# Three norm stages of a two-part transformer kernel: the second weight unit of the next block is cast later, and its early pieces move behind the last transpose

## The chip, the cores and the metric

The kernel runs on one core of a Trainium2 chip. The metric is the device time of one execution in microseconds (us), lower being better. A core has a matrix engine (TensorE, in the rows PE, its weight loads PEld), a vector engine (VectorE, DVE), a scalar engine (ScalarE, ACT), a general engine (GpSimd, POOL), and SyncE (SP), whose queue issues the weight loads here.

## The reference, cut to what matters

Everything is float32, one batch of 512 tokens of width 1024. Two layers of a mixed block (gated recurrence, latent attention, cross-attention, layer norm) come first. The second part is one block of this form, and the change lies in it:

```python
f = swiglu(rms_norm(h, ffn1_pre_g[i]), ffn1_w_gate[i], ffn1_w_up[i], ffn1_w_down[i])
h = h + 0.5 * rms_norm(f, ffn1_post_g[i])
m = hybrid_mixer(rms_norm(h, mix_pre_g[i]), w_in[i], ...)
h = h + rms_norm(m, mix_post_g[i])
f = swiglu(rms_norm(h, ffn2_pre_g[i]), ffn2_w_gate[i], ffn2_w_up[i], ffn2_w_down[i])
h = h + 0.5 * rms_norm(f, ffn2_post_g[i])
e = (p[i] @ ple_w_proj[i]) * jax.nn.sigmoid(rms_norm(h, ple_pre_g[i]) @ ple_w_gate[i])
```

After the first feed-forward, after the mixer and after the second feed-forward the same thing happens: the sum over a token's 1024 values is squared and averaged, h is updated, h is squared and averaged again, scaled, and multiplied by the next weights.

## The kernel before, in words

**Matmuls.** A float32 product is made of three matmuls of split operands: each operand is a rounded high part (`xh`, `wh`) and the rest (`xl`, `wl`), and lines 867 to 869 issue high by high, low by high and high by low. Weights come in units of up to four tiles of 128x512. For each unit SyncE loads `raw` (line 797, two buffers, so that the load of unit u waits until the low parts of unit u-2 are made), ScalarE casts the four tiles to `wh` (line 1200, three buffers, so that the cast of unit u waits until TensorE is through with unit u-3), and GpSimd makes `wl` as raw minus wh (line 816, one instruction for each tile). A block of weights of 1024 rows is two units; a piece is one unit by one PSUM bank, 12 matmuls. Only the first piece of a unit waits for the low tiles, one by one.

**Norm stages.** `norm_order` writes out by hand the order in which TensorE, ScalarE and VectorE go through such a stage; a `Phase("norm")` carries it. There are five: mode "layer" closes each of the two layers of the first part, and mode "post" stands behind the first feed-forward, behind the mixer and behind the second feed-forward. The change touches mode "post"; below, the first, second and third stage are these three. For each of the four groups t of 128 tokens it goes: the last two down pieces (`part`) on TensorE, their sum (`evac`, line 1571) and the gain product (`gain`, line 1895) on VectorE, a square with root (`root`, lines 1457 and 1458) on ScalarE, the update of h (`x`, line 1906) on VectorE, a second square with root (`root2`, lines 1464 and 1465) on ScalarE, the scaling in two halves (`n`, line 1914) on VectorE, the transposes of the two halves (`t`, line 1105, four each) on TensorE, and the split of the transposed values into `xh` (`high`, lines 1472 and 1475) and `xl` (`low`, lines 1924 and 1930).

**Pieces ahead.** The block that follows the stage (`next_block`) is begun within it: its pieces over the first 256 tokens need only t = 0 and 1. These are in `early`, eight pieces of 12 matmuls with 256 columns where the block is of kind "tr" (behind the first feed-forward and behind the mixer), and four pieces with 512 columns where it is "nat" (behind the second feed-forward). They are dealt out in three lots (`lots`): behind the last down piece, behind the transposes of t = 2, and behind those of t = 3. I call the block's two units A and B; the first half of `early` uses A, the second half B. The second token half of the block follows, for A and then B again.

**Casts ahead.** `("units", 0)` and `("units", 1)` in ScalarE's order are the casts of A and of B, four tiles each. In ScalarE's order the steps of t = 3 read, before the change: units 1 (B's casts), root 3, high 2, root2 3, high 3.

Of the kernel before, what the change touches and what calls it, by code (L numbers as in the profile page):

```python
# [216 lines left out]
def norm_order(first, pre, turned):  # L217

    last = T - 1
    if not turned:
        pe = [("part", t, n) for t in range(T) for n in range(2)]
        act = [("root", t) for t in range(T)]
        dve = sum(([("evac", t, 0, 2), ("gain", t), ("x", t)] for t in range(T)), [])
    else:
        def turn(t):
            return [("t", t, b) for b in range(2)]

        def high(t):
            return [("high", t, b) for b in range(2)]

        def low(t):
            return [("low", t, b) for b in range(2)]

        def n(t):
            return [("n", t, b) for b in range(2)] if pre else []

        def root2(t):  # L240
            return [("root2", t)] if pre else []

        parts = [[("part", t, b)] for t in range(T) for b in range(2)]
        early = [[("early", i)] for i in range(3)]
        if first == "layer":

            parts = [[("part", t, b)] for t in range(T) for b in range(4 if t == 1 else 2)]
            pe = parts[:7] + [turn(0), parts[7], parts[8], turn(1), parts[9], early[0], turn(2), early[1], turn(3), early[2]]

            def evac(t, a, b):  # L250
                return [("evac", t, a, b)]

            def ready(t):
                return [("stat", t), ("gain", t)]

            def x(t):
                return [("x", t)]

            def root(t):
                return [("root", t)]  # L260

            dve = [evac(0, 0, 2), ready(0), evac(1, 0, 1), x(0), evac(1, 1, 2), n(0), evac(1, 2, 4), ready(1), x(1),
                   evac(2, 0, 1), low(0), n(1), evac(2, 1, 2), ready(2), evac(3, 0, 1), x(2), low(1), evac(3, 1, 2),
                   ready(3), n(2), x(3)]
            dve += [n(3), low(2), low(3)] if pre else [low(2), low(3)]
            act = [root(0), root2(0), [("units", 0)], root(1), high(0), root2(1), root(2), high(1), root2(2), root(3),
                   [("units", 1)], root2(3), high(2), high(3)]
        else:
            pe = parts[:5] + [turn(0), parts[5], parts[6], turn(1), parts[7], early[0], turn(2), early[1], turn(3), early[2]]
            act, dve = [[("units", 0)]], []  # L270
            for t in range(T):
                dve.append([("evac", t, 0, 2)])
                if t:
                    dve.append(n(t - 1))
                dve.append([("gain", t), ("x", t)])
                if t:
                    dve.append(low(t - 1))
                act.append([("units", 1), ("root", t)] if t == last else [("root", t)])
                if t:
                    act.append(high(t - 1))  # L280
                act.append(root2(t))
            dve += [n(last), low(last)]
            act.append(high(last))
        pe, act, dve = (sum(order, []) for order in (pe, act, dve))
    free = ("part", "early", "evac", "units")
    at = [{k: i + 1 for i, k in enumerate(k for k in order if k[0] not in free)} for order in (pe, act, dve)]
    return (pe, act, dve), at


def build(nc, x, x_t, mem_t, positions, w_in, w_uq, w_uk, w_uv, w_mk, w_mv, w_out, ln_g, ln_b, cols_in,  # L290
# [3 lines left out]
    with ctx:  # L294
# [105 lines left out]
        def w_cols(w, row0, ktiles, c0, width):  # L400
            return w[row0:row0 + ktiles * P, c0:c0 + width].rearrange("(k p) n -> p k n", p=P)
# [17 lines left out]
        def norm(first, last_blocks, pre=None, turned=True, scale=1.0, second=True, by_columns=False):  # L419


            _, at = norm_order(first, pre, turned)
            ph = Phase("norm", *(len(o) for o in at), slots=T + 1, writes="x" if turned else None, mode=first,
                       gain=pre, tiles=2 if turned else 0, scale=scale, layer=second)
            ph.by_columns = by_columns
            if len(last_blocks) == 2:
                last_blocks[1].shift = 2
            if first == "layer":

                between, *ends = (b.pieces() for b in last_blocks)  # L430
                for b, at in zip(last_blocks, ((0, 1, 0, 1), (2, 2, 0, 2), (3, 3, 1, 3))):
                    b.shift, b.at = 0, at
                ph.slots[0], ph.slots[2] = between[:2], between[2:]
                for n in range(T):
                    ph.slots[n + 1] += [pieces[n] for pieces in ends]
                add(ph)
                return
            for b in last_blocks:
                pieces = b.pieces()
                ph.slots[0] += pieces[:-T]  # L440
                for n in range(T):
                    ph.slots[n + 1].append(pieces[n - T])
            add(ph)
# [143 lines left out]
        for n in range(2):  # L587
            add(blk2(2048 + 512 * n, "nat", "sigmoid", "act", SG2) if n else rest)
            add(Block(w_cols(w_ba, 0, 4, n * 512, 512), 4, 512, "nat", "y", "merge", "dve", (n, True, SG2)))
            if n == 0:  # L590
# [5 lines left out]
        last = [Block(w_cols(w_out2, k * 512, 4, n * 512, 512), 4, 512, "nat", "x", "accumulate", "dve", (n, k == 0))  # L596
                for k in range(2) for n in range(2)]
# [46 lines left out]
        units, unit_end, bank_user = [], [], {}  # L644
# [67 lines left out]
        for u, (_, _, nk) in enumerate(units):  # L712
            for k in range(nk):
                lows[low_on_dve(u, k)] += 1
                low_at[u, k] = lows[low_on_dve(u, k)]
            low_upto.append(tuple(lows))

        tiles_upto = [0]
        for _, _, nk in units:
            tiles_upto.append(tiles_upto[-1] + nk)  # L720
# [100 lines left out]
        def _(pe):  # L821
# [55 lines left out]
            def half_pieces(b, half):  # L877

                return [pc for pc in b.pieces() if b.kind != "nat" or pc[2] // 2 == half]
# [5 lines left out]
            for e in plan:  # L885
# [142 lines left out]
                elif e.kind == "level" and e.level <= LEVELS:  # L1028
                    for h in range(4):
# [3 lines left out]
                        for c in range(T):  # L1033
# [6 lines left out]
                            for o in range(0, P, 64):  # L1040
                                own = slice(c * P + o, c * P + o + 64)
                                right, n = Q[:, h, own], 64
                                if e.level:
                                    right, n = right.rearrange("p (b two i) -> p b two i", two=2,
                                                               i=2 ** (e.level - 1))[:, :, 1, :], 32
# [19 lines left out]
                elif e.kind == "read_out":  # L1065
                    for c in range(T):
# [6 lines left out]
                        mm.then_inc(pe_step, 1)  # L1073
                elif e.kind == "norm":
                    (order, _, _), (_, act_at, dve_at) = norm_order(e.mode, e.gain, e.tiles)
                    early = half_pieces(e.next_block, 0) if e.tiles else []
                    n = len(early) // 4
                    first = 2 * n if e.mode == "layer" else n
                    lots = early[:first], early[first:3 * n], early[3 * n:]

                    def half_written():

# [3 lines left out]
                    for key in order:  # L1086
                        if key[0] == "part":
                            _, t, n = key
# [7 lines left out]
                        _, t, b = key  # L1096
# [63 lines left out]
        def _(act):  # L1160
# [79 lines left out]
            for e in plan:  # L1240
# [187 lines left out]
                elif e.kind == "hg_norm":  # L1428
                    act.activation(stat[:, 16:32], stat[:, 0:16], ACT.Sqrt, bias=col("eps_rms"),
                                   scale=1 / P).then_inc(act_step, 1)  # L1430
                elif e.kind == "norm":
                    (_, order, _), (pe_at, act_at, dve_at) = norm_order(e.mode, e.gain, e.tiles)
                    squares = square2_out if e.layer else square_out
                    if e.mode == "layer":
# [666 lines left out]
```

## Time and profile before

| what | value |
| --- | --- |
| time, median of 3 runs | 2168.9 us (2168.37 to 2169.25) |
| profiled execution: its own time | 2171.62 us |
| profiled execution: span | 2169.8 us |
| TensorE busy | 2134.5 us, 98% of the span |
| GpSimd busy | 877.0 us, 40% |
| mean granted TensorE clock | 0.997 of full |

The span is from the first to the last instruction of one profiled execution; its own time, 1.8 us longer, has what lies around it. Times in rows are counted from the start of the span. "Idle before" is how long the engine stood before the row and what ended it.

### The profile page before, as it was taken

Reading aid. Unit: us, or ns where it says so; the run is one execution under the profiler, and the core shown is the slowest. Engines: PE = TensorE matmul, PEld = TensorE weight load, DVE = VectorE, ACT = ScalarE, POOL = GpSimd, SP = SyncE. Lnnn points to the kernel's source line nnn. Section 1 sums busy time; section 2 is a strip of 40 time slices with the busy share of each in tenths; the row PEclk is TensorE's granted clock in tenths of the full one; section 3 lists DMA queues with packets and bytes.
Section 4 is the critical chain, followed back from the end, with each engine's and each line's share of the span. In section 5 each row is a group of like instructions: output and inputs, shape, how many; then the busy total and the mean of one; then the engine's idle time right before and its main releaser. Section 6 shows DMA issues by size and latency. Waiting matters only on the chain. (4 is left out here: it accounts for less than half of the span.)

```text
span 2169.8 us, 30402 instructions
## 1 busy us (share of the span) xinstructions
PE 2134.5 (98%) x12268; PEld 1756.7 (81%) x12268; DVE 880.0 (41%) x1669; ACT 787.7 (36%) x1609; POOL 877.0 (40%) x688
## 2 busy tenths in 40 slices
PE   7999999999999999999999999999999999999998
PEld 7888888778888888678888888887788888888876
DVE  6074464535355374534531212353432532222264
ACT  4413325454324224445522222244523432222245
POOL 4533433232443433223453544434354345454433
PEclk9999999999999999999999999999999999999999
DMA  6422222112321212113142322322132223332222
GB/s 244 156 77 79 75 65 94 43 61 77 97 79 59 94 56 68 59 59 107 50 146 78 117 97 78 112 98 88 59 117 97 78 81 123 107 99 97 96 68 87
DMA packets 98667, 196.45 MB, mean 91 GB/s; under 512 B 3680, under 2 KB 12256, under 8 KB 98144
## 3 DMA queue, kind: packets, MB, share of 16 engines
q1 hardware_dynamic: 95072, 183.25, 25.7%
q10 hardware_dynamic: 3456, 11.27, 1.5%
q8 instruction: 97, 1.59, 0.3%
q14 instruction: 42, 0.34, 0.1%
HBM read 192.41 MB, written 2.10 MB: 90 GB/s over the span
## 5 line engine op out<-in xcount | busy, mean ns | idle before, releaser
L816 POOL TENSOR_TENSOR wl<-raw,wh 128x512 fp32r<-128x512 f32 (+2 forms) x684 | 876.8, 1305 | 1265.9 <-ACT wh L1200 1255.9
L1200 ACT CAST wh<-raw 128x512 fp32r<-128x512 f32 (+2 forms) x692 | 380.2, 603 | 768.2 <-PE ps L869 669.8
L867 PE MATMUL ps<-xh,wh 128*128 128x512 f32 (+1 forms) x1376 | 516.2, 375 | 3.9 <-POOL wl L816 2.6
L869 PE MATMUL ps<-xh,wl 128*128 128x512 f32 (+1 forms) x1376 | 509.9, 371 | 0.0
L868 PE MATMUL ps<-xl,wh 128*128 128x512 f32 (+1 forms) x1376 | 509.5, 370 | 0.0
L867 PEld LDWEIGHTS ps<-xh,wh 128*128 128x128 f32 x1376 | 260.1, 189 | 50.5 <-issue 4.6
L869 PEld LDWEIGHTS ps<-xh,wl 128*128 128x128 f32 x1376 | 259.9, 189 | 44.6
L868 PEld LDWEIGHTS ps<-xl,wh 128*128 128x128 f32 x1376 | 260.2, 189 | 42.1
L867 PE MATMUL ps<-wh,xh 128*128 128x512 f32 (+1 forms) x608 | 240.1, 395 | 0.2 <-issue 0.2
L869 PE MATMUL ps<-wh,xl 128*128 128x512 f32 (+1 forms) x608 | 234.8, 386 | 0.0
L868 PE MATMUL ps<-wl,xh 128*128 128x512 f32 (+1 forms) x608 | 234.7, 386 | 0.0
L867 PE MATMUL ps<-wh,yh 128*128 128x512 f32 x496 | 199.6, 402 | 2.1 <-DVE side L1555 2.0
L869 PE MATMUL ps<-wh,yl 128*128 128x512 f32 x496 | 194.4, 392 | 0.0
L868 PE MATMUL ps<-wl,yh 128*128 128x512 f32 x496 | 194.2, 392 | 0.0
L1575 DVE TENSOR_TENSOR work<-ps,work 128x512 f32<-128x512 f32 x44 | 30.3, 688 | 381.1 <-PE ps L869 381.1
L867 PEld LDWEIGHTS ps<-wh,xh 128*128 128x128 f32 x608 | 114.2, 188 | 23.3 <-issue 1.9
L869 PEld LDWEIGHTS ps<-wh,xl 128*128 128x128 f32 x608 | 114.2, 188 | 21.7
L868 PEld LDWEIGHTS ps<-wl,xh 128*128 128x128 f32 x608 | 114.3, 188 | 20.4 <-issue 0.2
L867 PEld LDWEIGHTS ps<-wh,yh 128*128 128x128 f32 x496 | 93.9, 189 | 22.4 <-ACT xh L1289 2.1
L869 PEld LDWEIGHTS ps<-wh,yl 128*128 128x128 f32 x496 | 93.6, 189 | 20.0
L868 PEld LDWEIGHTS ps<-wl,yh 128*128 128x128 f32 x496 | 93.6, 189 | 18.4
L1571 DVE TENSOR_TENSOR side<-side,ps 128x512 f32<-128x512 f32 x88 | 59.3, 686 | 106.0 <-PE ps L869 103.4
(261 smaller groups left out, 2460.6 us busy)
## 6 DMA issues: line engine op xcount, KB each, us to landing
raw<-w_in SPq DMA_DIRECT2D x58, 1024.0 KB, 5.2
raw<-w_out SPq DMA_DIRECT2D x20, 1024.0 KB, 5.1
raw<-f1g SPq DMA_DIRECT2D x10, 1024.0 KB, 5.1
raw<-f1u SPq DMA_DIRECT2D x10, 1024.0 KB, 5.1
raw<-f1d SPq DMA_DIRECT2D x10, 1024.0 KB, 5.1
raw<-f2g SPq DMA_DIRECT2D x10, 1024.0 KB, 5.1
raw<-f2u SPq DMA_DIRECT2D x10, 1024.0 KB, 5.1
raw<-f2d SPq DMA_DIRECT2D x10, 1024.0 KB, 5.1
```

Source lines behind the costliest of these rows:

```text
L816: pool.tensor_tensor(wl[s], raw[:, u % 2, k, 0:b.width], wh[s].bitcast(F32), ALU.subtract).then_inc(low_done, 1)
L867: pe.matmul(o, still[0], move[0], start=k0 + k == 0, stop=False)
L868: pe.matmul(o, still[0], move[1], start=False, stop=False)
L869: mm = pe.matmul(o, still[1], move[0], start=False, stop=k0 + k == b.ktiles - 1)
L1200: act.copy(wh[:, v % 3, k, 0:width], raw[:, v % 2, k, 0:width]).then_inc(high_done, 1)
L1571: ins = dve.tensor_copy(dst, src) if first else dve.tensor_tensor(dst, dst, src, ALU.add)
L1575: link(dve.tensor_tensor(tmp, src, SG[:, j, :], ALU.mult))
```

## The change

In mode "post", B's casts go from ahead of root 3 to behind root2 3, directly ahead of high 3. The lots of `early` were one, two and one quarters of the pieces and are now one, one and two quarters: all of B's pieces stand behind the transposes of t = 3. Mode "layer" keeps its order and its lots.

```diff
-                act.append([("units", 1), ("root", t)] if t == last else [("root", t)])
+                act.append([("root", t)])
                 if t:
                     act.append(high(t - 1))
                 act.append(root2(t))
             dve += [n(last), low(last)]
-            act.append(high(last))
+            act += [[("units", 1)], high(last)]
...
                     first = 2 * n if e.mode == "layer" else n
-                    lots = early[:first], early[first:3 * n], early[3 * n:]
+
+                    second = 3 * n if e.mode == "layer" else 2 * n
+                    lots = early[:first], early[first:second], early[second:]
```

## Rows read from the trace of the kernel before

**Rows 1.** The page: busy us by engine; one costly group (busy us, mean ns)

```profile
PE 2134.5 (98%) x12268; PEld 1756.7 (81%) x12268; DVE 880.0 (41%) x1669; ACT 787.7 (36%) x1609; POOL 877.0 (40%) x688
...
L1571 DVE TENSOR_TENSOR side<-side,ps 128x512 f32<-128x512 f32 x88 | 59.3, 686 | 106.0 <-PE ps L869 103.4
```

**Rows 2.** Waits of TensorE, whole span: us in total, times, longest

```profile
PE ps L1105 <- DVE work L1914: 4.5, 6, 1.0
```

**Rows 3.** Timeline, first stage, ScalarE: start us, duration us, instruction, [idle before]

```profile
1424.17 0.29 ACT L1465 ACTIVATE stat<-stat,cols 128x1 f32<-128x1 f32 x1
1424.37 2.17 ACT L1200 CAST wh<-raw 128x512 fp32r<-128x512 f32 x4
1433.07 1.06 ACT L1464 ACTIVATE work<-xs 128x1024 f32<-128x1024 f32 x1 [3.08 <-DVE xs L1906]
1434.25 0.29 ACT L1465 ACTIVATE stat<-stat,cols 128x1 f32<-128x1 f32 x1
```

**Rows 4.** Timeline, first stage, VectorE, t = 2, then t = 3

```profile
1420.34 1.22 DVE L1895 TENSOR_TENSOR work<-side,work 128x1024 f32<-128x1024 f32 x1
...
1421.67 1.28 DVE L1906 SCALAR_TENSOR_TENSOR xs<-work,stat,xs 128x1024 f32<-128x1024 f32 x1
...
1426.82 1.77 DVE L1914 SCALAR_TENSOR_TENSOR work<-xs,stat,work 128x512 f32<-128x512 f32 x1
1428.51 2.29 DVE L1895 TENSOR_TENSOR work<-side,work 128x1024 f32<-128x1024 f32 x1
...
1430.92 2.12 DVE L1906 SCALAR_TENSOR_TENSOR xs<-work,stat,xs 128x1024 f32<-128x1024 f32 x1
```

**Rows 5.** Timeline, first stage, GpSimd: one low tile, four, the next four

```profile
1426.30 1.74 POOL L816 TENSOR_TENSOR wl<-raw,wh 128x512 fp32r<-128x512 f32 x1
...
1425.05 6.91 POOL L816 TENSOR_TENSOR wl<-raw,wh 128x512 fp32r<-128x512 f32 x4 [18.51 <-ACT wh L1200]
1440.63 5.01 POOL L816 TENSOR_TENSOR wl<-raw,wh 128x512 fp32r<-128x512 f32 x4 [8.67 <-ACT wh L1200]
```

**Rows 6.** Timeline, first stage, TensorE: transposes of t = 2 and 3

```profile
1428.64 0.66 PE L1105 MATMUL ps<-ident,work 128*128 128x128 f32 x4 [0.71 <-DVE work L1914]
...
1435.59 1.32 PE L1105 MATMUL ps<-ident,work 128*128 128x128 f32 x8 [0.63 <-DVE work L1914]
...
1439.51 0.28 PE L869 MATMUL ps<-xh,wl 128*128 128x256 f32 x1
```

**Rows 7.** Timeline, second stage: n 2, root2 3, transposes of t = 3

```profile
1734.00 3.02 DVE L1914 SCALAR_TENSOR_TENSOR work<-xs,stat,work 128x512 f32<-128x512 f32 x2
...
1742.68 0.29 ACT L1465 ACTIVATE stat<-stat,cols 128x1 f32<-128x1 f32 x1
...
1744.02 1.32 PE L1105 MATMUL ps<-ident,work 128*128 128x128 f32 x8 [0.55 <-DVE work L1914]
```

**Rows 8.** Timeline, third stage and the casts behind it

```profile
2102.01 3.01 DVE L1914 SCALAR_TENSOR_TENSOR work<-xs,stat,work 128x512 f32<-128x512 f32 x2
...
2112.04 1.32 PE L1105 MATMUL ps<-ident,work 128*128 128x128 f32 x8 [0.81 <-DVE work L1914]
2115.74 0.39 PE L869 MATMUL ps<-wh,xl 128*128 128x512 f32 x1
...
2124.79 1.65 ACT L1200 CAST wh<-raw 128x512 fp32r<-128x512 f32 x3
...
2126.62 0.39 PE L869 MATMUL ps<-wh,xl 128*128 128x512 f32 x1
2127.18 0.47 PE L867 MATMUL ps<-wh,yh 128*128 128x512 f32 x1 [0.18 <-issue]
```

**Rows 9.** Waits of TensorE, 1055 to 1070 us, the layer norm stage

```profile
PE ps L867 <- POOL wl L816: 1.7, 2, 1.1
```

**Rows 10.** Windows there: stretch, us; busy us of PE, PEld, DVE, ACT, POOL; clock, DMA, GB/s

```profile
1060.00:1064.00 4.00, 2.70 (x21) 2.25 (x19) 2.42 (x4) 2.40 (x5) 4.00 (x3) 1.00 0.00 0
1064.00:1068.00 4.00, 3.64 (x18) 3.64 (x19) 2.05 (x3) 0.00 (x0) 0.30 (x1) 0.57 0.61 193
```

## The prediction, made before the change was run

> **What bounds the kernel now.** I read the page's busy times first: TensorE is busy for 98% of the span, GpSimd for 40% [rows 1]. So a gain can only come out of TensorE's waits, and a new wait of TensorE goes straight into the time. Its waits come next: 4.5 us in six waits of line 1105, the transposes, for line 1914, the scaling `n`, two in each of the three stages that the change touches [rows 2]. That is about all the change could win. Then I read the first stage engine by engine. VectorE's second half of `n` 2, `gain` 3 and `x` 3 take 1.77, 2.29 and 2.12 us, though `gain` and `x` took 1.22 and 1.28 us for the group of tokens before [rows 4]. In the same stretch GpSimd makes B's four low tiles, in 6.91 us where the next four take 5.01 [rows 5]. The two hold each other up, one instruction of the one for one of the other. TensorE meanwhile works through pieces of A and B and waits 0.71 us and 0.63 us for the transposes of t = 2 and t = 3 [rows 6]. Between t = 3's transposes and the second token half lie two pieces of B, until 1439.51 + 0.12 = 1439.6.
>
> **What the change removes.** B's casts (2.17 us of ScalarE, from 1424.37 [rows 3]) no longer start GpSimd next to `n` 2, `gain` 3 and `x` 3. Without that company `n` 2 from 1425.71 takes 1.4 us as the pair does when GpSimd is still, `gain` follows at 1427.04, `x` at 1428.37 and ends at 1429.65, against 1430.92 + 2.12 = 1433.04 now. Root 3 isn't in the way: VectorE's sum of t = 3 is there at 1425.5, a square with root takes 1.47 us from start to end (1433.07 to 1434.25 + 0.29 = 1434.54 [rows 3]), so it is ready at 1427.0. Root2 3, which ended at 1434.54, ends at 1429.67 + 1.47 = 1431.14. Call this moment R. It is 3.4 us earlier than now. This alone would look like a gain, but the gain can be no larger than the waits that TensorE has there.
>
> **What the change adds.** The casts now begin at R. Before, GpSimd's first tile began 0.68 us after the first cast (1425.05 against 1424.37 [rows 3, 5]), which itself began 0.1 us ahead of the end of the root; so GpSimd starts at R + 0.6. It runs beside `n` 3, which starts at R + 0.24. The first half of `n` 3 holds GpSimd's first tile until R + 0.95, this ends at R + 2.1, the second half of `n` 3 waits for it and ends at R + 2.7 (1.77 us from its start, as the row of `n` 2 has it [rows 4]), and GpSimd's second tile takes 1.74 us as in the row [rows 5]. The third and fourth take 5.01 / 4 = 1.25 us each, since `low` 3 reads PSUM and one SBUF tensor and should not meet GpSimd: the sums of line 1571 have the same kind of inputs, lie beside low tiles all through the kernel, and have a mean of 0.69 us [rows 1]. The low tiles stand at R + 2.1, 3.8, 5.05 and 6.3. On ScalarE `high` 3 is now behind the casts, to R + 2.1; the first transposes of t = 3 are through at R + 1.7, so `high` 3 is 0.4 us late, and `low` 3 ends near R + 4.8. Who waits for it is the second token half, due at R + 11, and in the first and third stage a gains load behind it; none of them notices. SyncE's queue: the load into the raw buffer that B's low tiles free goes out at R + 6.3 = 1437.4 instead of 1432.0, and its cast needs TensorE to be through with A, at 1448, so the load has 10 us to land. GpSimd's next four tiles, 1440.6 to 1445.6 now [rows 5], come at 1438 to 1443 because the gains load goes out earlier.
>
> The skill bears on the one point where VectorE and GpSimd meet. The rows show alternation, tile by tile [rows 4, 5]. The Trainium skill (SBUF — State Buffer, Who interferes with whom) says that a VectorE instruction with two SBUF inputs and a GpSimd instruction that reads SBUF block each other for a whole instruction, and one with a single SBUF input doesn't; by this rule, the trace agrees, and the sum stays as it is.
>
> **TensorE, first stage.** A piece of 12 matmuls with 256 columns takes 1.43 us (0.12 us a matmul). Before, the eight early pieces had waits of 1.34 us among them. After: the piece for the last down product and A's first two pieces end at 1427.3; the transposes of t = 2, now without a wait, at 1428.4; A's other two at 1431.3. The first half of t = 3's transposes can start at R + 1.05 = 1432.2 (a wait of 0.9), the second at R + 2.75 = 1433.9 (a wait of 1.1). Then B's first piece takes each low tile as it comes: the fourth at R + 6.3 + 0.1, and three matmuls more, 1437.9; it could have been through at 1435.9, a wait of 2.0. Three pieces more end at 1442.2, against 1439.6. **First stage: +2.6 us** (4.0 us of waits for 1.34).
>
> **Second stage.** The same sum from its rows: `n` 2 starts at 1734.00, so `x` 3 ends at 1737.94 and R is 1739.4 against 1742.97 [rows 7]. Early pieces end at R + 11.1 = 1750.5. Before they ended as long after the transposes (1744.02 [rows 7]) as in the first stage, 4.05 us, at 1748.05. **+2.45 us.**
>
> **Third stage.** The pieces have 512 columns, 2.73 us each, and only two are B's. `n` 2 starts at 2102.01 [rows 8], R is 2107.4. B's first piece ends at R + 6.4 + 0.7 = 2114.5, its second at 2117.25. Before, the one that stood there ended at 2115.74 + 0.16 = 2115.9 [rows 8]: +1.35. Something comes back: ahead of the projection TensorE now loses about 0.5 us (2126.62 to 2127.18, and once more after it, where 0.23 is usual [rows 8]), because ScalarE's casts come only at 2124.79; these hang on a chain of gains loads that starts with `low` 3, which comes 2.5 us earlier. **+0.85 us.**
>
> Sum: 2.6 + 2.45 + 0.85 = 5.9 us. No later wait takes it back: between the stages TensorE's list of waits has one, for a copy of ScalarE's that itself follows TensorE. Where the extra wait goes, everything behind it, a pure TensorE stretch, is late by the same amount.
>
> **The clock.** The layer norm stage, which has B's casts late already, shows what this pattern does. TensorE waited twice, 1.7 us in all, for B's low tiles [rows 9], and then the granted clock was 0.57 over 1064 to 1068 [rows 10], that is mostly at 1.2 instead of 2.4 GHz. What is lost at full speed is 4 x (1 - 0.57) = 1.7 where all of it is work, and 0.3 us of it were idle (busy 3.64 of 4) [rows 10]. I call it 1.4 us. The changed stages have longer waits. The bounds are nothing (the slow stretch lies where TensorE waits for GpSimd anyway) and 1.4 us in each of three stages. I take 0.3 us for each, because most of the slow stretch should lie on the waits: +0.9. The Trainium skill (TensorE: Matmul & The Clock Gate, HAM oscillation) ties the fall to long idle gaps of TensorE; none here is over 1.3 us, and by it the clock would hold and the sum stay at 5.9. The rows of the layer norm stage speak against it.
>
> The sum is made on an execution whose own time was 2171.6 us, 2.7 above the median of the runs; the difference is put on the median: 2168.9 + 5.9 + 0.9 = 2175.7.
>
> **The rivals.** (1) *The early end of `x` wins: faster.* R comes 3.4 us earlier and TensorE gets back what it waits for `n`. This needs B's first piece to end by 1439.6 - 4.3 = 1435.3, R + 4.2, so four low tiles within 3.3 us of GpSimd's start. They take 5.0 us with nobody beside them [rows 5]. If it held, at most the 4.5 us of waits go [rows 2]: 2164.4. From a tile of 0.8 us on it decides. Chance 4%. (2) *Within 0.2%:* 0.2% is 4.3 us, about what a measurement of this kernel tells from no change. GpSimd isn't held up at all (0.65 us less in each stage) and TensorE's clock holds: 5.9 - 1.95 = 3.95, so 2172.9. It needs the alternation not to happen beside `n` 3. Chance 14%. (3) *The clock falls on the full pieces:* the slow stretch begins late, as at 1064, and covers work; 5.9 + 3 x 1.4 = 10.1, 2179.0. For it: the layer norm stage lost it all. Against: there the low tiles were through when the clock fell. It is the upper end of my forecast's own case. Chance 17%. (4) *The low tiles don't gate because TensorE is late anyway:* then only transposes' waits count, 0.9 + 1.1 against 1.34, +0.7 in each of the first two stages: 2170.5. It needs TensorE to arrive at B's first piece after R + 5; it arrives at R + 3.4. Chance 3%, within 0.2% too.
>
> **How the numbers follow.** Forecast 2175.7 with 62%. The range reaches from (2)'s neighbourhood, 2172.2, to 2179.0. Faster by over 0.2% 0.04; within 0.2% 0.17 (rivals 2 and 4); slower by over 0.2% 0.79 (forecast and rival 3).
>
> **What would show it.** Right: `n` 2, `gain` 3 and `x` 3 back at 1.4, 1.2 and 1.3 us in all three stages; GpSimd's four tiles starting 0.6 us behind root2 3; new waits of TensorE for line 816, about 2 us in each of the first two stages and less in the third, and a wait of 1 us between the two halves of t = 3's transposes; a granted clock below 1 in some of these stages. Wrong: if line 816 doesn't appear as a releaser there, or if the four low tiles take far less than 5 us.

## The result

The changed kernel takes 2176.4 us (median of 6 runs, 2175.42 to 2176.85), the kernel before 2169.75 us (6 runs): a ratio of 1.0031, 95% interval 1.0018 to 1.0044. That is slower by 6.6 us. The forecast was 6.8 us (2175.7 from 2168.9).

The profiled execution of the changed kernel has a span of 2174.1 us and an own time of 2175.9 us. Its list of TensorE's waits over the whole span shows more time in the six waits for line 1916 (6.2 us; it is `n`, line 1914 before, 4.5 us in [rows 2]) and four more waits for GpSimd (first two lines: changed; third line: before; us in total, times, longest):

```profile
PE ps L867 <- POOL wl L816: 12.6, 10, 7.8
PE ps L1107 <- DVE work L1916: 6.2, 6, 1.2
```

```profile
PE ps L867 <- POOL wl L816: 10.4, 6, 7.2
```

The chain on VectorE did get faster. These rows are the second stage, VectorE then ScalarE (start, duration); `gain` 3 and `x` 3 have 1.22 and 1.28 us instead of what [rows 4] shows for the first stage, and the root behind `x` 3 ends 5.46 us behind the start of `n` 2 instead of 8.97 [rows 7]:

```profile
1734.66 1.42 DVE L1916 SCALAR_TENSOR_TENSOR work<-xs,stat,work 128x512 f32<-128x512 f32 x2
1735.99 1.22 DVE L1897 TENSOR_TENSOR work<-side,work 128x1024 f32<-128x1024 f32 x1
...
1737.32 1.28 DVE L1908 SCALAR_TENSOR_TENSOR xs<-work,stat,xs 128x1024 f32<-128x1024 f32 x1
...
1739.83 0.29 ACT L1467 ACTIVATE stat<-stat,cols 128x1 f32<-128x1 f32 x1
1740.03 2.16 ACT L1202 CAST wh<-raw 128x512 fp32r<-128x512 f32 x4
```

With R = 1739.83 + 0.29 = 1740.12, GpSimd's tiles there, one by one, and the second half of `n` 3, which lies on the first tile:

```profile
1740.70 1.53 POOL L816 TENSOR_TENSOR wl<-raw,wh 128x512 fp32r<-128x512 f32 x1 [24.78 <-ACT wh L1202]
1741.02 1.76 DVE L1916 SCALAR_TENSOR_TENSOR work<-xs,stat,work 128x512 f32<-128x512 f32 x1
1742.19 1.73 POOL L816 TENSOR_TENSOR wl<-raw,wh 128x512 fp32r<-128x512 f32 x1
1743.88 1.27 POOL L816 TENSOR_TENSOR wl<-raw,wh 128x512 fp32r<-128x512 f32 x1
1745.12 1.27 POOL L816 TENSOR_TENSOR wl<-raw,wh 128x512 fp32r<-128x512 f32 x1
```

The tiles end at R + 2.1, 3.8, 5.0 and 6.3. And TensorE in the same stretch, where it stands four times (the first two in the transposes of t = 3, the others in B's first piece):

```profile
1741.16 0.66 PE L1107 MATMUL ps<-ident,work 128*128 128x128 f32 x4 [0.96 <-DVE work L1916]
1742.84 0.66 PE L1107 MATMUL ps<-ident,work 128*128 128x128 f32 x4 [1.02 <-DVE work L1916]
1743.25 0.36 PE L867 MATMUL ps<-xh,wh 128*128 128x256 f32 x1
...
1743.97 0.39 PE L867 MATMUL ps<-xh,wh 128*128 128x256 f32 x1
...
1745.21 0.39 PE L867 MATMUL ps<-xh,wh 128*128 128x256 f32 x1 [0.61 <-POOL wl L816]
...
1746.45 0.39 PE L867 MATMUL ps<-xh,wh 128*128 128x256 f32 x1 [0.62 <-POOL wl L816]
```

A listed wait is less than the time lost. Between 1745.21 and 1746.45 three matmuls of 0.12 us are done in 1.24 us, so 0.88 us are lost and 0.62 us listed. B's first piece as a whole goes from 1743.25 to about 1746.8, 3.6 us where 1.43 us would do: 2.1 us lost, 1.2 us listed.

**How a stage is measured below.** Two profiled executions are not the same until the stage begins: the transposes of t = 1 in the first stage began at 1420.1 before and at 1416.6 after. In the kernel before, the granted clock was at half for some 3 us near 50 us and again in the layer norm stage [rows 10], in this execution of the changed kernel in neither; here is the layer norm stage of the changed kernel in the columns of [rows 10]:

```profile
1064.00:1068.00 4.00, 4.00 (x36) 4.00 (x35) 1.34 (x3) 3.10 (x6) 1.43 (x2) 1.00 0.67 247
```

So I compare lengths: from the first transpose of t = 1 to the first matmul behind the second token half of the next block, always 228 matmuls in stages one and two, 132 in stage three (start times of these two matmuls in each trace; numbering them works, as every trace has 12268). "Half clock" says that the granted clock was at 1.2 GHz, the lower of its two levels, for part of the stage.

| kernel | first | second | third | over before | half clock in |
| --- | --- | --- | --- | --- | --- |
| before | 31.06 | 31.25 | 30.54 | | none |
| changed | 35.22 | 33.76 | 31.98 | +8.1 | first, third |
| changed, second profile | 33.69 | 33.78 | 31.99 | +6.6 | third |
| casts late, old lots | 35.58 | 36.23 | 32.43 | +11.4 | all |
| new lots, old casts | 36.18 | 36.64 | 34.51 | +14.5 | all |
| changed, half low tiles | 31.53 | 31.59 | 29.83 | +0.1 | none |
| casts behind root 3 | 31.70 | 33.28 | 29.80 | +1.9 | second |
| casts behind high 1 | 30.25 | 30.50 | 29.52 | -2.6 | none |
| casts behind root 2 | 30.17 | 30.30 | 29.28 | -3.1 | none |

### The profile page after: what moved, and what is told of

Its sections match the earlier page's. It is cut to its first block and busy times, and to the rows that moved or that the text cites. A ratio compares the mean times of both kernels' runs of the same rounds, so it can differ in the third digit from the quotient of the medians.

```text
span 2174.1 us, 30402 instructions
## 1 busy us (share of the span) xinstructions
PE 2136.2 (98%) x12268; PEld 1757.6 (81%) x12268; DVE 873.2 (40%) x1669; ACT 787.6 (36%) x1609; POOL 873.3 (40%) x688
```

## The experiments

### Each half of the change alone

The first has the new place of the casts and the lots of before (cut from its difference to the changed kernel):

```diff
-                    second = 3 * n if e.mode == "layer" else 2 * n
+                    second = 3 * n
```

> Only the first half of the change: B's casts behind the second square of t = 3, the lots as before (two of B's pieces, in the third stage one, ahead of the transposes of t = 3). My theory (TensorE waits for GpSimd's four low tiles of B, which begin 0.6 us behind the second root and take 5.7 us): B's first piece still ends about 6.8 us behind that root, and now the transposes of t = 3 stand behind it and no longer fill the wait, so each of the first two stages costs 1.1 us more than with the whole change: about 3.7 + 3.5 + 1.9 = 9 us over the kernel before, 10 with the clock. Rival (what costs is that B's pieces were taken away from between the transposes of t = 2 and t = 3): the time is that of the kernel before within 2 us.

It took 2181.6 us against 2170.3, a ratio of 1.0057 (1.0044 to 1.0069): +11.2 us, where 9 to 10 were expected. The rival is out. In its trace the third stage is 1.9 us longer, as I had it; the first two are 4.5 and 5.0 us longer instead of 3.7 and 3.5, with a half clock in each. Its waits of TensorE in the second stage (total, times, longest) are for GpSimd, but for one of 0.4 us that names no engine, where the changed kernel has 2.0 us in the transposes and 1.2 us for GpSimd:

```profile
PE ps L867 <- POOL wl L816: 3.6, 4, 2.1
```

The second has the new lots and the casts of before (again against the changed kernel):

```diff
-                act.append([("root", t)])
+                act.append([("units", 1), ("root", t)] if t == last else [("root", t)])
...
-            act += [[("units", 1)], high(last)]
+            act.append(high(last))
```

> Only the second half of the change: all of B's pieces behind the transposes of t = 3, B's casts ahead of the first square of t = 3 as before. My theory: the scaling, the gain and the update still share the stretch with GpSimd, so the second root of t = 3 ends as late as before, and TensorE, out of pieces 2.9 us earlier (2.7 in the third stage), waits about 3.5 us for the transposes of t = 3 instead of 0.6; +2.8 +2.8 +2.2 = 8 us over the kernel before, and a granted clock below 1 behind the wait. No wait for line 816. Rival (the late low tiles are the whole cost): the time of the kernel before within 2 us.

It took 2183.5 us, a ratio of 1.0063 (1.0050 to 1.0075): +13.1 us, and its rival is out too. In its second stage TensorE waits 3.4 us in one piece for the scaling of t = 3, as expected, and never for line 816:

```profile
PE ps L1107 <- DVE work L1916: 4.3, 2, 3.4
```

I had said 8 us and a clock below 1, without a price for it. The excess is the clock, which stood at half for a part of all three stages, for about 7 us in each of the first two. In the second stage the transposes of t = 3 begin 15.7 us behind the first transpose of t = 1, as in the kernel before, and the early pieces end 9.4 us later. Before, those eight transposes and the two pieces behind them took 4.0 us at full clock; with two more pieces of 1.43 us that makes 6.9. So of the 5.4 us that this stage is longer, 2.9 are the missing pieces, as expected, and 2.5 the clock. Each half alone is worse than both together. The casts late make the low tiles late, and the lots then put the transposes into the wait; the lots alone leave TensorE with nothing to do.

### Is it GpSimd's low tiles?

The changed kernel, but the low parts of B's right half of the columns are left out, so that a tile is 256 wide:

```diff
+            halved = [e.next_block.unit_ids[1] for e in plan
+                      if isinstance(e, Phase) and e.kind == "norm" and e.mode == "post" and e.tiles]
...
-                    s = (slice(None), u % 3, k, slice(0, b.width))
-                    pool.tensor_tensor(wl[s], raw[:, u % 2, k, 0:b.width], wh[s].bitcast(F32),
+                    width = b.width // 2 if u in halved else b.width
+                    s = (slice(None), u % 3, k, slice(0, width))
+                    pool.tensor_tensor(wl[s], raw[:, u % 2, k, 0:width], wh[s].bitcast(F32),
```

> The whole change, but GpSimd makes the low parts of only the left half of the columns of B's four tiles in the three stages (left out: the low parts of the right half), so that a tile takes about 0.65 us. My theory: B's first piece ends 4.6 us behind the second root instead of 6.8, and the transposes' second half follows the first sooner; some 2 us come back in each stage, so 0.5 to 1.5 us over the kernel before. Rival (TensorE is short of pieces between the transposes, and the clock falls for that): at most 2 of the 6.6 us come back.

2170.56 us against 2170.34 before, a ratio of 1.0001 (0.9992 to 1.0010, which is 1.7 us less to 2.2 us more): the 6.6 us are gone within that interval, and the rival is out. I had expected 0.5 to 1.5 us over the kernel before, and the interval holds that too. In its second stage no wait for the low tiles is left, and the two for the scaling are shorter, since the second half of `n` 3 takes 1.22 us beside the narrow tiles instead of 1.76:

```profile
PE ps L1110 <- DVE work L1919: 1.5, 2, 1.0
```

The clock fell in none of its stages. GpSimd's time for B's four tiles, behind the second root of t = 3, is what the change costs. The experiment takes away together what hangs on that time: the waits of B's first piece, the hold on `n` 3, and the half clock; it doesn't part them.

### The clock, in a second profile of the changed kernel

> The changed kernel once more, for the clock. My theory: the three stages take 2.5, 2.5 and 0.8 us more than before where the granted clock holds, and up to 1.7 us more where it falls; which of them it falls in isn't the same in each execution. Rival: the first stage costs 4.2 us by its waits, in every execution.

Its time was 2175.2 us. The first stage is 33.69 us instead of 35.22, and the granted clock is what differs. Stages one and two cost 2.6 and 2.5 us more than before here, which is what I expected for a clock that holds, and the rival (4.2 us by the waits alone) is out. First the windows of the first profile from 1430 on, then the same place of the second (columns as [rows 10]):

```profile
1430.00:1434.00 4.00, 3.21 (x13) 2.62 (x13) 1.83 (x5) 0.93 (x4) 3.95 (x3) 0.58 0.05 4
1434.00:1438.00 4.00, 4.00 (x20) 4.00 (x21) 0.00 (x0) 2.18 (x4) 2.95 (x3) 0.56 0.98 363
```

```profile
1429.00:1433.00 4.00, 2.30 (x14) 1.65 (x14) 3.31 (x6) 2.72 (x7) 3.94 (x3) 1.00 0.01 2
1433.00:1437.00 4.00, 2.85 (x21) 2.65 (x22) 0.31 (x1) 2.14 (x4) 3.16 (x4) 1.00 0.63 197
```

The order of work is the same and so are the times up to the fall (to 0.1 us, counted from the first transpose of t = 1); the clock fell once and once not. The windows at 0.58 and 0.56 would lose 3.4 us if all of them were work; they cost 1.5 us here. I take it, without a test, that the rest fell where TensorE would have stood for GpSimd's tiles. In the second stage it fell in neither profile, in the third in both, near 2113:

```profile
2113.00:2117.00 4.00, 3.65 (x11) 3.09 (x12) 1.59 (x3) 0.77 (x2) 3.90 (x3) 0.57 0.04 6
```

### Where should the casts stand?

Three other places in ScalarE's order, all with the lots of before; each cut is a difference to the kernel before. One step later than before, behind root 3:

```diff
-                act.append([("units", 1), ("root", t)] if t == last else [("root", t)])
+                act.append([("root", t), ("units", 1)] if t == last else [("root", t)])
```

> One place in ScalarE's order later than before: B's casts directly behind the first square of t = 3, the lots as before. My theory: GpSimd's tiles begin about 2.5 us later than before, meet gain 3, x 3 and n 3 instead of n 2, gain 3 and x 3; the second root of t = 3 ends about 2.4 us earlier than before, but B's first piece, which stands ahead of the transposes of t = 3, waits for its fourth tile until about 1435 in the first stage's clock of before: 0.9 us more in each of the first two stages, 2 to 3 us over the kernel before in all. Rival (what counts is only when VectorE's steps of t = 3 end): up to 1.5 us less than before.

2172.7 us against 2169.7, a ratio of 1.0012 (1.0003 to 1.0021): +3.0 us, at the upper end of the 2 to 3 expected; the rival is out. Its profile has 0.6 and 2.0 us more in the first two stages, the 2.0 with a half clock. Of the engines its list for the second stage names only GpSimd, and no transpose waits. The third stage is 0.7 us shorter, for which the expectation names no figure.

```profile
PE ps L867 <- POOL wl L816: 1.7, 2, 1.1
```

One step earlier than before, behind high 1:

```diff
-                act.append([("units", 1), ("root", t)] if t == last else [("root", t)])
+                act.append([("root", t)])
                 if t:
                     act.append(high(t - 1))
+                if t == 2:
+                    act.append([("units", 1)])
```

> A version meant to beat both: the lots as before, B's casts earlier than before, behind the split of t = 1 and ahead of the second square of t = 2. GpSimd's first two tiles then lie beside the low parts of t = 1 and the sums of t = 3, which read PSUM, and only the scaling of t = 2 meets it; gain and update of t = 3 run alone. My theory (VectorE and GpSimd hold each other up only where VectorE has two SBUF inputs): the second root of t = 3 is 1.4 us earlier than before, the wait for its transposes (0.6 us) goes, that of t = 2 stays or grows by 0.3: 0.3 to 0.6 us less in each stage, 1 to 1.8 us less in all. Rival (the company only moves, and the second square of t = 2 is late by the casts): no change, or up to 1 us more.

2169.4 us against 2170.3, a ratio of 0.9995 (0.9986 to 1.0004): not told apart from no change by the time (3.0 us less to 0.9 us more). The stages are 0.8, 0.75 and 1.0 us shorter in its trace, 2.6 in all, more than the 1 to 1.8 expected, while the median is only 1.0 us lower; no run shows where the rest goes. VectorE's `n` 2 takes longer than before, both halves lie on GpSimd tiles, and `gain` 3 and `x` 3 run alone (first stage):

```profile
1424.29 3.13 DVE L1916 SCALAR_TENSOR_TENSOR work<-xs,stat,work 128x512 f32<-128x512 f32 x2
1427.35 1.21 DVE L1897 TENSOR_TENSOR work<-side,work 128x1024 f32<-128x1024 f32 x1
...
1428.67 1.28 DVE L1908 SCALAR_TENSOR_TENSOR xs<-work,stat,xs 128x1024 f32<-128x1024 f32 x1
```

Two steps earlier, directly behind root 2:

```diff
-                act.append([("units", 1), ("root", t)] if t == last else [("root", t)])
+                act.append([("root", t), ("units", 1)] if t == 2 else [("root", t)])
```

> Two places earlier than before: B's casts directly behind the first square of t = 2, ahead of the split of t = 1, the lots as before. My theory: GpSimd begins 1.5 us earlier than in the version with the casts behind the split of t = 1, so only one half of n 2 meets it instead of two, but x 2 meets it once, and the split of t = 1 is 1.7 us late, for which TensorE's first piece of A waits 0.5 to 1 us more. The two about cancel: the three stages together 1 to 3 us shorter than before, the time 1 to 2 us less. Rival (the late split is paid in full, since everything of A waits for it): 1 to 3 us more than before.

2166.3 us against 2169.7, a ratio of 0.9987 (0.9978 to 0.9996): 3.4 us less than before (0.9 to 4.8), where 1 to 2 were expected, and it beats both kernels; the rival is out. `n` 2 now takes 2.11 us for both halves; `x` 2 meets GpSimd once:

```profile
1418.96 2.13 DVE L1906 SCALAR_TENSOR_TENSOR xs<-work,stat,xs 128x1024 f32<-128x1024 f32 x1
...
1423.84 2.11 DVE L1914 SCALAR_TENSOR_TENSOR work<-xs,stat,work 128x512 f32<-128x512 f32 x2
1425.87 1.21 DVE L1895 TENSOR_TENSOR work<-side,work 128x1024 f32<-128x1024 f32 x1
```

No transpose is waited for any more. What is left in the first stage is one wait ahead of A's first piece, for the split of t = 1 (the trace names no releaser; A's first piece waits for `high` and `low` of t = 1 by the code, and `low` 1 ends just then):

```profile
PE ps L867 <- issue: 1.3, 1, 1.3
```

## Why the prediction was right

**The chain on VectorE: right.** `gain` 3 and `x` 3 take 1.22 and 1.28 us in the changed kernel, and R comes 5.46 us behind the start of `n` 2 where the sum had 5.4.

**The low tiles: right to 0.1 us.** R + 2.1, 3.8, 5.05, 6.3 were said; 2.1, 3.8, 5.0, 6.3 are in the rows of the second stage. The 2 us that B's first piece should lose there are 2.1 us. The half-width experiment shows that they carry the cost. Rival 1 needed four tiles within 3.3 us and they took 5.7; even 256 columns wide they take 3.5 us, and the kernel is only back to where it was.

**First and second stage: right, one load by luck.** +2.6 and +2.45 us were worked out for a clock that holds; +2.63 (second profile) and +2.5 (both) were measured. I had given the load that B's low tiles let go in the first stage 10 us and asked no more. Beside two loads of 1024 KB on ScalarE's queue (into `side`) it took 11.0 us, where it took 5.2 before:

```profile
raw<-w_in SPq DMA_DIRECT2D x1, 1024.0 KB, 11.0
```

Issued at 1433.97 it landed at 1445.0, and the cast that needs it began at 1446.33, still released by TensorE. That is a margin of 1.3 us which the prediction didn't know of.

**Third stage: the total about right, the give-back for a wrong reason.** I had +1.35 for the stage and 0.5 back ahead of the projection, because `low` 3 and with it the chain of gains loads would start 2.5 us earlier. Up to the last matmul of the second token half, 31.76 us behind the first transpose of t = 1, the stage is 1.8 us longer (29.98 before), in both profiles with a half clock in it. Then 0.7 us come back, half of it at the next matmul, where the stages in the table end, the other half just behind. To the last matmul of the kernel it is 64.4 us against 63.3, so +1.1 against +0.85.

The half clock is about 0.5 us of the 1.8. These are the fourth low tile and the first matmul that needs it, in the changed kernel:

```profile
2115.62 1.27 POOL L816 TENSOR_TENSOR wl<-raw,wh 128x512 fp32r<-128x512 f32 x1
...
2117.50 0.39 PE L867 MATMUL ps<-wh,xh 128*128 128x512 f32 x1
```

The tile ends at 2116.9 and the matmul starts 0.6 us later; in the second stage it started within 0.1 us of the tile's end (1746.45 against 1745.12 + 1.27). TensorE was late by its own clock, and the wait for line 816 that I had expected in this stage isn't in its list.

The give-back was of about the right size, and that is luck: the chain is not early. The first of the load issues starts 2.1 us sooner, and then these loads meet the load into the raw buffer that B's low tiles free, which before was through: issued at 2108.4, landed in 5.1 us. Now it goes out at 2116.9. The landing times of the three in the changed kernel (KB each, median us to landing), and below them those before:

```profile
raw<-ple_gate SPq DMA_DIRECT2D x1, 1024.0 KB, 7.2
work<-post_gains ACTq DMA_DIRECT2D x1, 512.0 KB, 4.5
work<-p_t ACTq DMA_DIRECT2D x1, 512.0 KB, 4.9
```

```profile
raw<-ple_gate SPq DMA_DIRECT2D x1, 1024.0 KB, 5.1
work<-post_gains ACTq DMA_DIRECT2D x1, 512.0 KB, 3.6
work<-p_t ACTq DMA_DIRECT2D x1, 512.0 KB, 3.6
```

The casts behind them start 28.3 us behind the first transpose of t = 1, before 28.15. The 0.7 us come back all the same, because TensorE itself arrives later. I had looked at the moved load in the first stage and left it out in this one.

**The clock: the term of about the right size, for a reason only half right.** +0.9 us over three stages was the estimate. The two profiles of the changed kernel show 1.5 us in the first stage once and nothing once, nothing in the second, and about 0.5 us in the third in both: 2.0 and 0.5 us in all, not 0.3 in each stage. The kernel loses its clock in some executions and not in others, and that moves single profiles against each other. All nine run the same order up to the first stage, and yet the first transpose of t = 1 comes at 1416.2 to 1417.4 us in the three with no fall of the clock before it and at 1420.1 and 1420.6 in the two with two falls. What decides it within one order of work wasn't tested. On the rule of the Trainium skill (TensorE: Matmul & The Clock Gate, HAM oscillation), which ties the fall to long idle gaps, the runs are against that reading: in the stages of the changed kernel it fell with no listed wait of TensorE over 1.2 us near.

**Rivals.** Rival 1 (faster) and 2 (GpSimd not held up beside `n` 3) failed on the rows of tiles above: 1.53 and 1.73 us for the two that meet `n` 3, 1.27 us for the others. Rival 3 (1.4 us for the clock in each stage, 2179.0 us) failed too: no run of the changed kernel took over 2176.9 us, and no fall came in the second stage. Rival 4 asked that TensorE come to B's first piece after R + 5; it came at R + 3.1.

## What to carry to other kernels

Moving work away from a chain that it slows down is worth at most what the bounding engine waits for that chain, here 4.5 us, and the moved work has a consumer of its own: count from its new start to its last result, and set that beside the moment at which the bounding engine arrives. If two engines hold each other up, look for the stretch in which one of them has instructions of the kind that doesn't meet the other, and put the work there. Here that was earlier, not later: two places earlier took 3.4 us off, one place earlier nothing that the times can tell, one place later added 3.0. And when a step frees a buffer later, look at which other loads the refill now meets.

## What the runs showed of the hardware

A VectorE instruction with two SBUF inputs and GpSimd's low tiles take turns, one for one: tiles of 1.25 us become 1.73 us and scalings of 0.75 us become 1.76 us, where one meets one; beside a 1024 wide instruction of VectorE a tile takes 2.27 us. `low` 3 with one SBUF input and PSUM takes 0.69 us beside a tile of 1.28 us, so neither holds the other. In seven kernels with whole tiles the four of the first stage took from 5.6 to 7.0 us according to what lay beside them (6.91 before, 5.68 changed, 5.64 casts late with old lots, 6.91 new lots with old casts, 5.77 behind high 1, 6.41 behind root 2, 6.97 behind root 3).

The granted clock fell to 1.2 GHz beside two waits of TensorE of 1.0 to 1.2 us each in the changed kernel, and beside one wait of 3.4 or 3.5 us in the version with new lots and old casts. In the first stage of the changed kernel it fell in one execution and not in the next. It stayed there for some 3 or some 7 us.

A load of 1024 KB landed in 5.1 or 5.2 us with none beside it in these traces, in 7.2 us beside two of 512 KB that followed one another, and in 11.0 us beside two of 1024 KB and one of 256 KB.
